# The MLP of a decoder layer in two phases, its down-projection as seven block products

## The chip, the cores and the metric

The kernel runs on one core of one Trainium2 chip. The metric is the device time of one execution in microseconds (us); 1 MB is a million bytes. Engine names are those of the profile: PE is TensorE, DVE is VectorE, ACT is ScalarE, POOL is GpSimd and SP is SyncE, which here issues almost all DMAs.

## What is computed

One layer of a decoder on x of 1024 tokens by 1024 features in float32: four token mixers, merged by gates and projected, are added to x, then the MLP is:

```
h = rms_norm(x, g_mlp) * (1 + sc2) + sh2          # (1024, 1024)
x = x + gt2 * (square(relu(h @ w_up)) @ w_down)   # w_up (1024, 4096), w_down (4096, 1024)
```

The change touches only the MLP. Below, u is square(relu(h @ w_up)), the hidden matrix.

## The kernel before

Every float32 product is made from two parts of each operand: a high part (ACT copies the float32 tile to fp32r, the format that PE reads) and a low part (operand minus high part, by DVE). `split_product` (L658) issues three matmuls for each pair of 128-row tiles: high by high, high by low, low by high, each with 128x128 weights and 512 moving columns.

All of the MLP is in `stage_close` (L676). The hidden features are cut into NB = 16 blocks of two tiles (BF = 2) of 128. For each block b there is an up-projection and a down-projection:

- Up, blocks 0 and 1 ("plain", 192 matmuls for both): a block's four results (feature tile f, token half h) are plain products.
- Up, blocks 2 to 15: seven products P1 to P7 take the place of eight (Winograd's form of Strassen's scheme), 12 matmuls each, 84 for a block. They need sums of w_up's quarters (`sum_units`, L1347, DVE, four 128x512 operations) and sums of h, made once (`difference`, nine DVE operations of 128x2048, and `low_difference`, four). `combine` (L1447) adds the products up from PSUM with five DVE operations.
- Down, every block: `down` (L1253) multiplies u's block by w_down's block as plain products, 16 groups (column half c, token tile tt) of 6 matmuls, 96 for a block. After each group `accumulate` (L1513) adds one 128x512 PSUM bank to x1, which is resident in SBUF. The gain gt2 is multiplied into w_down's tiles beforehand (`scale_unit`).

PE's order is: plain(0), plain(1), and then for b = 0..15 down(b) followed by up(b + 2) while there is one. The orders of ACT, DVE and SP are written out by hand to match. PSUM has eight banks; four serve the up products and four the down groups. w_up and w_down tiles of 256 KB pass through eight `unit` buffers, and their two parts through six slots. u stays in SBUF and is used by the next down(b). POOL does nothing in the MLP: its last work, the low parts of w_in's tiles (`Dense.low`, L137), ends before the MLP. SP stores each finished half row of x1 during the last block.

Of the kernel before, what the change touches and what calls it, by code (L numbers as in the profile page):

```python
# [675 lines left out]
def stage_close(nc, k, dense, w_br, x, w_out, w_up, w_down, out):  # L676
# [9 lines left out]
    with ExitStack() as ctx:  # L686

        def at(name, kb, shape, dt=F32):
# [33 lines left out]
        square = at("tl_square", 32, [P, BF, NH, HALF])  # L722
        first_product = at("tl_first_product", 216, [P, HALF])
        u_hi = [at("tl_u_hi", 48, [P, BF, S], F32R), at("tl_u_hi_last", 72, [P, BF, S], F32R)]
        u_lo = [at("tl_u_lo", 56, [P, BF, S], F32R), at("tl_u_lo_last", 80, [P, BF, S], F32R)]
        gain2 = at("tl_gain2", 40, [P, D])
        ps_y = ctx.enter_context(nc.psum_tensor("mg_ps_y", [P, Y_RING, NH, HALF], F32))
# [11 lines left out]
         turned, weighted, shifted, h_hi_ready, h_lo_ready, t_step, t_hi_ready, t_lo_ready, unit_scaled, unit_summed, slot_hi_ready, slot_lo_ready,  # L739
         up_done, taken, combined, relu_ready, square_ready, u_hi_ready, u_lo_ready, down_done, summed, out_stored) = sems(  # L740
# [3 lines left out]
                "t_lo_ready", "unit_scaled", "unit_summed", "slot_hi_ready", "slot_lo_ready", "up_done", "taken", "combined", "relu_ready",  # L744
                "square_ready", "u_hi_ready", "u_lo_ready", "down_done", "summed", "out_stored")))
# [3 lines left out]
        P1, P6, P5, P7, P2, P3, P4 = range(7)  # L749
        ITEMS = [("plain", b, (f, kh)) for b in range(PLAIN) for f in range(BF) for kh in range(2)]  # L750
        for b in range(NB):
            ITEMS += [("down", b, (c, f)) for c in range(NH) for f in range(BF)]
            if b + PLAIN < NB:
                ITEMS += [("up", b + PLAIN, (p,)) for p in range(7)]
        FIRST_DOWN = 4 * PLAIN
# [2095 lines left out]
```

## Time and profile before

| what | value |
|---|---|
| device time, median of three runs | 2024.57 us |
| the three runs | 2020.14, 2024.57, 2024.82 us |
| span of the profiled execution, first to last instruction | 2020.5 us |
| own device time of the profiled execution | not recorded beside its span |
| PE busy | 1967.2 us (97%), 9416 matmuls |
| DVE busy | 1264.0 us (63%) |
| ACT busy | 706.4 us (35%) |
| POOL busy | 227.3 us (11%) |
| DMA | 206.47 MB, mean 102 GB/s |

The span is that of one execution and is compared with spans of timelines; the runs are timed from outside it. Busy shares are averages over a program whose stages have different limits, so a share says little of the MLP by itself.

### The profile page before, as it was taken

The page shows a single profiled execution, that of the slowest core. Times are in us where ns is not written, and L with a number is a line of the kernel's source. Part 1 is how long each engine was busy: PE and PEld are TensorE (multiplying, and loading weights), DVE is VectorE, ACT ScalarE, POOL GpSimd, SP SyncE. Part 2 cuts the span into 40 slices and gives each one's busy share as a digit, 9 for nine tenths or more (in the row PEclk, how much of TensorE's full clock was granted, in tenths as well). Part 3 has the DMA queues.
Part 4 walks back from the last instruction along what each step waited for, and adds up shares of the span by engine and source line. Part 5 has one row for each costly group of instructions (what it writes and reads, how often), then busy time and mean ns, then how long its engine had stood idle before and what let it go on. Part 6 is the DMA issues. An engine that isn't in the chain of part 4 may idle for free. (4 is left out here: it accounts for less than half of the span.)

```text
span 2020.5 us, 24310 instructions
## 1 busy us (share of the span) xinstructions
PE 1967.2 (97%) x9416; PEld 1584.5 (78%) x9416; DVE 1264.0 (63%) x1655; ACT 706.4 (35%) x1100; POOL 227.3 (11%) x136
## 2 busy tenths in 40 slices
PE   5999999999999999999999999999999999999999
PEld 4787888878766677877788788787888888888887
DVE  6546666101356476548457587669877777777776
ACT  5411212123466542166654443333232122222221
POOL 0121212112222144121101000000000000000000
PEclk9999999999999999999998999999999999999999
DMA  8354554224311252353122765301111111211112
GB/s 275 96 150 144 160 153 141 89 83 123 123 58 47 68 169 58 105 209 120 47 75 83 257 229 182 115 11 59 57 52 60 47 47 48 68 48 48 48 42 94
DMA packets 197339, 206.47 MB, mean 102 GB/s; under 512 B 9402, under 2 KB 154938, under 8 KB 197226
## 3 DMA queue, kind: packets, MB, share of 16 engines
q1 hardware_dynamic: 197056, 204.85, 32.1%
q8 instruction: 76, 1.25, 0.3%
q14 instruction: 37, 0.30, 0.0%
q10 hardware_dynamic: 170, 0.07, 0.0%
HBM read 157.57 MB, written 47.32 MB: 101 GB/s over the span
## 5 line engine op out<-in xcount | busy, mean ns | idle before, releaser
L663 PE MATMUL dn_ps<-h_hi,dn_hi 128*128 128x512 f32 (+1 forms) x1120 | 453.0, 404 | 15.2 <-PEq L60 4.8
L665 PE MATMUL dn_ps<-h_hi,dn_lo 128*128 128x512 f32 (+1 forms) x1120 | 439.7, 393 | 0.0
L664 PE MATMUL dn_ps<-h_lo,dn_hi 128*128 128x512 f32 (+1 forms) x1120 | 439.5, 392 | 0.0
L663 PEld LDWEIGHTS dn_ps<-h_hi,dn_hi 128*128 128x128 f32 (+1 forms) x1120 | 210.5, 188 | 83.2 <-issue 32.6
L665 PEld LDWEIGHTS dn_ps<-h_hi,dn_lo 128*128 128x128 f32 (+1 forms) x1120 | 210.4, 188 | 47.6
L139 POOL TENSOR_TENSOR dn_lo<-dn_raw,dn_hi 128x1024 fp32r<-128x1024 f32 (+1 forms) x69 | 172.4, 2499 | 661.6 <-ACT dn_hi L135 661.6
L664 PEld LDWEIGHTS dn_ps<-h_lo,dn_hi 128*128 128x128 f32 (+1 forms) x1120 | 210.7, 188 | 43.2 <-issue 1.2
L1521 DVE TENSOR_TENSOR tl_x<-tl_x,mg_ps_y 128x512 f32<-128x512 f32 x256 | 176.0, 688 | 89.4 <-PE mg_ps_y L665 82.7
L156 ACT ACTIVATE dn_out<-dn_ps 128x512 f32<-128x512 f32 (+1 forms) x138 | 81.8, 592 | 422.7 <-PE dn_ps L665 401.6
L663 PE MATMUL mg_ps_y<-tl_slot_hi,tl_u_hi 128*128 128x512 f32 x480 | 187.1, 390 | 1.2 <-issue 1.2
L665 PE MATMUL mg_ps_y<-tl_slot_hi,tl_u_lo 128*128 128x512 f32 x480 | 186.9, 389 | 0.0
L664 PE MATMUL mg_ps_y<-tl_slot_lo,tl_u_hi 128*128 128x512 f32 x480 | 186.8, 389 | 0.0
L1021 ACT ACTIVATE tl_slot_hi<-tl_unit 128x512 fp32r<-128x512 f32 x128 | 77.7, 624 | 134.4 <-DVE tl_unit L1372 108.8
L555 DVE SCALAR_TENSOR_TENSOR ada_sum<-ada,cols,ada_sum 128x256 f32<-128x256 f32 (+1 forms) x140 | 105.6, 754 | 4.7
L663 PEld LDWEIGHTS mg_ps_y<-tl_slot_hi,tl_u_hi 128*128 128x128 f32 x480 | 90.1, 188 | 20.7 <-issue 2.0
L665 PEld LDWEIGHTS mg_ps_y<-tl_slot_hi,tl_u_lo 128*128 128x128 f32 x480 | 90.1, 188 | 18.7
L664 PEld LDWEIGHTS mg_ps_y<-tl_slot_lo,tl_u_hi 128*128 128x128 f32 x480 | 90.1, 188 | 18.6
L1377 DVE TENSOR_TENSOR tl_slot_lo<-tl_unit,tl_slot_hi 128x512 fp32r<-128x512 f32 x128 | 86.5, 689 | 24.8 <-ACT tl_slot_hi L1021 24.8
L1021 ACT ACTIVATE tl_slot_hi<-tl_unit_sum 128x512 fp32r<-128x512 f32 x42 | 26.5, 632 | 172.9 <-DVE tl_unit_sum L1360 146.9
L1071 ACT ACTIVATE tl_u_hi<-tl_square 128x512 fp32r<-128x512 f32 x60 | 33.3, 621 | 142.5 <-PE mg_ps_y L665 127.2
L561 DVE TENSOR_TENSOR mod<-ps_m,cols 128x2 f32<-128x2 f32 x24 | 3.5, 158 | 117.7 <-PE ps_m L474 117.7
L135 ACT ACTIVATE dn_hi<-dn_raw 128x1024 fp32r<-128x1024 f32 (+1 forms) x71 | 73.7, 1040 | 6.1 <-DMA dn_raw<-w_in_dram 6.1
(390 smaller groups left out, 3468.6 us busy)
## 6 DMA issues: line engine op xcount, KB each, us to landing
dn_raw<-w_in_dram SPq DMA_DIRECT2D x70, 512.0 KB, 4.4
ada<-w_ada_dram SPq DMA_DIRECT2D x24, 1024.0 KB, 7.9
proj<-dn_out SPq DMA_DIRECT2D x72, 256.0 KB, 2.3
logits<-dn_out SPq DMA_DIRECT2D x64, 256.0 KB, 2.3
tl_unit<-w_up_dram SPq DMA_DIRECT2D x64, 256.0 KB, 2.9
tl_unit<-w_down_dram SPq DMA_DIRECT2D x64, 256.0 KB, 2.8
mg_gate<-logits SPq DMA_DIRECT2D x19, 512.0 KB, 4.7
wa_qk<-proj SPq DMA_DIRECT2D x6, 1024.0 KB, 8.3
```

What stands on the lines that cost most here:

```text
L135: self.nc.scalar.activation(self.hi_at(j), self.raw_at(j), ACT.Copy).then_inc(self.hi_ready, 1)
L139: self.nc.gpsimd.tensor_tensor(self.lo_at(j), self.raw_at(j), self.hi_at(j).bitcast(F32), ALU.subtract).then_inc(self.lo_ready, 1)
L156: self.nc.scalar.activation(self.out[0:width, h, :], self.ps[0:width, h, :], ACT.Copy).then_inc(self.copied, 1)
L555: ins = nc.vector.scalar_tensor_tensor(out=total, in0=part, scalar=ck, in1=total, op0=ALU.mult, op1=ALU.add)
L561: last = nc.vector.tensor_tensor(k.mod[:, m:m + ADA_COLS], ps_m[:, m:m + ADA_COLS], k.cols[:, V_BADA + m:V_BADA + m + ADA_COLS], ALU.add)
L663: nc.tensor.matmul(out, w_hi[:, t, :], x_hi[:, t, :], start=begin, stop=False, skip_group_check=reopened)
L664: nc.tensor.matmul(out, w_hi[:, t, :], x_lo[:, t, :], start=False, stop=False, skip_group_check=reopened)
L665: mm = nc.tensor.matmul(out, w_lo[:, t, :], x_hi[:, t, :], start=False, stop=end, skip_group_check=reopened)
L1021: nc.scalar.activation(slot_hi[slot(j)][:, :, :], src, ACT.Copy).then_inc(slot_hi_ready, 1)
L1071: nc.scalar.activation(hidden_at(u_hi, b)[:, f, h * HALF:(h + 1) * HALF], square[:, f, h, :], ACT.Copy).then_inc(u_hi_ready, 1)
L1377: nc.vector.tensor_tensor(slot_lo[slot(j)][:, :, :], unit_at(kind, b, key), slot_hi[slot(j)][:, :, :].bitcast(F32), ALU.subtract).then_inc ...
L1521: nc.vector.tensor_tensor(x1[:, tt, cols], x1[:, tt, cols], bank(4 + n % 4), ALU.add).then_inc(summed, 1)
```

## The change

The MLP now runs in two phases, with a DRAM tensor `hidden` between them.

**Phase 1** is the whole up-projection, with no down groups between the blocks. PE goes from plain(1) straight to P1(2). The products of a block are issued in two parts, the second part (P2, P3, P4) one block later than the first, and two sets of four PSUM banks alternate by block. ACT makes the ReLU and the square (`finish`). DVE makes four sums S1 to S4 of each finished block's quarters (`sum_hidden`). SP stores three of the quarters and the four sums to `hidden` (`store_hidden`), seven tiles of 128x512 (256 KB each) a block.

**Phase 2** is the down-projection over u in two token halves and feature tiles in pairs, as seven block products for eight. Product i takes one of the seven stored matrices and one of w_down's quarters, of which some are turned in place into sums by DVE (`turn_down`, 64 operations). Each product has 16 steps, 112 steps in all, and a step is 4 token tiles by 3 matmuls. For step n:

- SP loads one 256 KB tile of `hidden` into one of three raw buffers, once the low part of step n - 3 is made, and loads the w_down cells that a later step needs.
- ACT makes both high parts, DVE the low part of the hidden tile, POOL the low part of the w_down cell. The parts sit in a ring of nine places, two for each step, so high parts may be made at most four steps ahead of PE.

PSUM is left only between products: ACT keeps three of them (`keep`), and DVE multiplies by gt2 and adds to x1 in `evict_down`, 60 operations in stretches of steps given by `EVICT_AT`, plus the last product at the end. `link` waits for the operation just issued. gt2's rows are saved to DRAM and read back in halves. There are no more `accumulate`, `scale_unit`, `square_relu` or `low_hidden` of the old kind.

The core of the diff:

```diff
+        RING_KB = (92, 208, 212, 16, 56, 60, 20, 44, 204)
+        ring_hi = [at(f"tl_ring_hi{i}", kb, [P, HALF], F32R) for i, kb in enumerate(RING_KB)]
+        raw_hidden = [at(f"tl_raw_hidden{i}", kb, [P, HALF]) for i, kb in enumerate((64, 66, 68))]
+        kept = at("tl_kept", 0, [P, 4, HALF])
...
+        for b in range(PLAIN, NB + 1):
+            ITEMS += [("up", b, (p,)) for p in FIRST_PART if b < NB]
+            ITEMS += [("up", b - 1, (p,)) for p in SECOND_PART if b > PLAIN]
...
+        DOWN = [(A11, W11), (A12, W21), (S2, W11), (S3, W12), (S1, W11), (S4, W22), (A22, W21)]
+        BY_EVEN = (0, 2, 3, 6)
+        STEPS = len(DOWN) * NB
+        LAST_STEPS = 4
+        SUMS_FROM = 14
...
+        NEEDS = sorted([(t, W11, t) for t in range(NB)] + [(NB + t, W21, t) for t in range(NB)]
+                       + [(SUMS_FROM + 2 * t, w, t) for t in range(NB) for w in (W22, W12)])
...
+        EVICT_AT = {36: (1, 0), 39: (1, 1), 42: (1, 2), 45: (1, 3), 52: (2, 0), 54: (2, 1), 56: (2, 2), 58: (2, 3),
+                    68: (3, 0), 71: (3, 1), 74: (3, 2), 77: (3, 3), 84: (4, 0), 86: (4, 1), 88: (4, 2), 90: (4, 3),
+                    100: (5, 0), 102: (5, 1), 104: (5, 2), 106: (5, 3)}
...
+            if m >= 9:
+                eng.wait_ge(step_done, (m - 9) // 2 + 1)
+            elif m in (4, 5):
+                eng.wait_ge(slot_lo_ready, PLACE["up", NB - 1, (P4,)] + 1)
...
+            def store_hidden(b):
+                sp.wait_ge(quad_ready[0], b + 1)
+                sp.dma_start(k.hidden[A11, b], square[b % 2][:, 0, 0, :]).then_inc(quads_stored[b % 2], 16)
+                sp.wait_ge(quad_ready[1], b + 1)
+                sp.wait_ge(quad_ready[3], b + 1)
+                sp.dma_start(k.hidden[A12:A22 + 1, b].rearrange("s p t -> p s t"), square[b % 2][:, 1]).then_inc(quads_stored[b % 2], 16)
+                sp.wait_ge(hidden_summed, 4 * (b + 1))
+                sp.dma_start(k.hidden[S1:S4 + 1, b].rearrange("s p t -> p s t"), hidden_sum[:, :, :]).then_inc(sums_stored, 16)
...
+                if n < 3:
+                    sp.wait_ge(slot_lo_ready, PLACE["up", NB - 2, (P3,)] + 1)
+                else:
+                    sp.wait_ge(ring_lo_ready, n - 2)
...
+            for b in range(PLAIN, NB):
+                if b >= PLAIN + 1 and b + 1 < NB:
+                    load_ups(b + 1)
+                store_hidden(b - PLAIN)
+            for n in range(3):
+                load_hidden(n)
+            loaded = 0
+            while loaded < 15:
+                load_cell(loaded)
+                loaded += 1
+            store_hidden(NB - 2)
+            load_gain(0)
+            for n in range(3, STEPS):
+                while loaded < len(NEEDS) and NEEDS[loaded][0] <= n + 2:
+                    load_cell(loaded)
+                    loaded += 1
+                if n == 9:
+                    store_hidden(NB - 1)
+                load_hidden(n)
+                if n == 30:
+                    load_gain(1)
+                if n in STORE_AT:
...
+            def high_hidden(n):
+                act.wait_ge(hidden_in[n % 3], 16 * (n // 3 + 1))
+                wait_ring(act, 2 * n)
+                nc.scalar.activation(ring_hi[2 * n % 9][:, :], raw_hidden[n % 3][:, :], ACT.Copy).then_inc(ring_hi_ready, 1)
...
+                wait_ring(act, 2 * n + 1)
+                nc.scalar.activation(ring_hi[(2 * n + 1) % 9][:, :], cell(w, t)[:, :], ACT.Copy).then_inc(cell_hi_ready, 1)
...
+            for n in range(3):
+                high_hidden(n)
+                high_cell(n)
+            finish(NB - 1, 0, 0)
+            high_hidden(3)
+            high_cell(3)
+            finish(NB - 1, 1, 0)
+            finish(NB - 1, 0, 1)
+            for n in range(4, STEPS):
+                high_hidden(n)
+                if n - 3 in (NB, 3 * NB, 5 * NB):
+                    keep((n - 3) // NB - 1)
+                high_cell(n)
 
         @block.gpsimd
...
+                pool.wait_ge(cell_hi_ready, n + 1)
+                r, own = (2 * n + 1) % 9, cell(DOWN[n // NB][1], n % NB)
+                nc.gpsimd.tensor_tensor(ring_lo[r][:, :], own[:, :], ring_hi[r][:, :].bitcast(F32), ALU.subtract).then_inc(cell_lo_ready, 1)
...
+            for n in range(STEPS):
+                low_cell(n)
...
+                pe.wait_ge(ring_lo_ready, n + 1)
+                pe.wait_ge(cell_lo_ready, n + 1)
+                a, w = 2 * n % 9, (2 * n + 1) % 9
+                return split_product(nc, down_bank(i, tt), ring_hi[a][:, cols].unsqueeze(1), ring_lo[a][:, cols].unsqueeze(1),
+                                     ring_hi[w][:, :].unsqueeze(1), ring_lo[w][:, :].unsqueeze(1), first=(t == 0 and i not in (2, 3, 5)),
+                                     last=(t == NB - 1), reopened=i in (2, 3, 5))
...
+            for n in range(STEPS - LAST_STEPS):
+                for tt in range(4):
+                    last = down(n, tt)
+                    if n % NB == NB - 1 and tt < 3:
+                        last.then_inc(bank_done, 1)
+                last.then_inc(step_done, 1)
+            for tt in range(4):
+                for n in range(STEPS - LAST_STEPS, STEPS):
+                    last = down(n, tt)
+                last.then_inc(bank_done if tt < 3 else step_done, 1)
...
+                elif i == 3 and part == 0:
+                    link(nc.vector.tensor_tensor(product, own, g0, ALU.mult))
+                elif i == 3 and part == 1:
+                    link(nc.vector.tensor_tensor(rows[2], rows[2], product, ALU.subtract))
+                elif i == 3 and part == 2:
+                    nc.vector.tensor_tensor(other, own, g1, ALU.mult).then_inc(even_read, 1)
+                    dve.wait_ge(even_read, tt + 1)
+                elif i == 3 and part == 3:
+                    link(nc.vector.tensor_tensor(rows[3], rows[3], other, ALU.subtract))
...
+            for n in (1, 2, 3):
+                difference(n)
             for kh in range(2):
                 low_slot("plain", 1, (0, kh))
+            for n in (4, 5):
+                difference(n)
             for kh in range(2):
                 low_slot("plain", 1, (1, kh))
             low_difference(0)
             difference(6)
             difference(7)
             difference(8)
+            low_difference(1)
+            for n in (1, 2, 3):
+                sum_units(PLAIN, n)
+            for p in (P1, P6):
+                low_slot("up", PLAIN, (p,))
+            low_difference(2)
+            sum_units(PLAIN, 4)
+            for p in (P5, P7):
+                low_slot("up", PLAIN, (p,))
             difference(9)
+            low_difference(3)
+            for b in range(PLAIN, NB + 1):
+                if b > PLAIN:
+                    low_slot("up", b - 1, (P2,))
+                if b > PLAIN + 1:
+                    combine(b - 2, 5)
+                    combine(b - 2, 4)
+                if b > PLAIN:
+                    low_slot("up", b - 1, (P3,))
+                    low_slot("up", b - 1, (P4,))
+                if b < NB:
+                    combine(b, 1)
+                sum_hidden(b - 2)
+                if b + 1 < NB:
+                    for n in (1, 2, 3):
+                        sum_units(b + 1, n)
+                    for p in (P1, P6):
+                        low_slot("up", b + 1, (p,))
+                    sum_units(b + 1, 4)
+                    for p in (P5, P7):
+                        low_slot("up", b + 1, (p,))
+                if b < NB:
+                    combine(b, 2)
+                    combine(b, 3)
+            for n in range(3):
+                low_hidden(n)
+            combine(NB - 1, 5)
+            combine(NB - 1, 4)
+            low_hidden(3)
+            sum_hidden(NB - 1)
+            for n in range(4, STEPS):
+                where = EVICT_AT.get(n)
+                if where:
+                    evict_down(*where, 0)
+                if 0 <= n - SUMS_FROM < 4 * NB:
+                    turn_down(n - SUMS_FROM)
+                if where:
+                    evict_down(*where, 1)
+                low_hidden(n)
+                if where:
+                    evict_down(*where, 2)
+                if where:
+                    evict_down(*where, 3)
+            for tt in range(4):
+                evict_down(6, tt, 0)
+                evict_down(6, tt, 1)
```

## Rows read from the trace of the kernel before

**Rows 1.** The page: busy time and share of the engines; granted clock by slice.
```profile
PE 1967.2 (97%) x9416; PEld 1584.5 (78%) x9416; DVE 1264.0 (63%) x1655; ACT 706.4 (35%) x1100; POOL 227.3 (11%) x136
...
PEclk9999999999999999999998999999999999999999
```

**Rows 2.** Who PE waited for, from 1300 us to the end.
```profile
PE mg_ps_y L1208 <- DVE tl_xn L1397: 2.1, 2, 1.5
PE mg_ps_y L663 <- issue: 1.2, 1, 1.2
```

**Rows 3.** Timeline of PE, end of the plain products, and the last matmul: start, duration.
```profile
1395.83 0.39 PE L665 MATMUL mg_ps_y<-tl_h_hi,tl_slot_lo 128*128 128x512 f32 x1
...
1400.59 0.39 PE L665 MATMUL mg_ps_y<-tl_h_hi,tl_slot_lo 128*128 128x512 f32 x1
1400.82 0.39 PE L663 MATMUL mg_ps_y<-tl_slot_hi,tl_u_hi 128*128 128x512 f32 x1
...
2016.97 0.39 PE L665 MATMUL mg_ps_y<-tl_slot_hi,tl_u_lo_last 128*128 128x512 f32 x1
```

**Rows 4.** Groups from 1380 us on: count, busy us and mean ns, idle before.
```profile
L1377 DVE TENSOR_TENSOR tl_slot_lo<-tl_unit,tl_slot_hi 128x512 fp32r<-128x512 f32 x122 | 82.6, 689 | 24.8 <-ACT tl_slot_hi L1021 24.8
L1021 ACT ACTIVATE tl_slot_hi<-tl_unit 128x512 fp32r<-128x512 f32 x122 | 74.2, 625 | 134.4 <-DVE tl_unit L1372 108.8 <-PE mg_ps_y L665 25.5
...
L1057 ACT ACTIVATE tl_square<-dn_ps 128x512 f32<-128x512 f32 x16 | 9.2, 579 | 0.0
L1445 DVE TENSOR_TENSOR tl_t_lo<-tl_t_full,tl_t_hi 128x2048 fp32r<-128x2048 f32 x4 | 9.1, 2287 | 0.0
```

**Rows 5.** Timeline of DVE after the last tile of h: start, duration.
```profile
1367.63 0.68 DVE L1478 TENSOR_TENSOR tl_square<-tl_square 128x512 f32<-128x512 f32 x1
1368.23 2.29 DVE L1425 TENSOR_TENSOR tl_t_full<-tl_h_hi 128x2048 f32<-128x2048 f32 x1
1370.43 2.29 DVE L1427 TENSOR_TENSOR tl_t_full<-tl_h_lo 128x2048 f32<-128x2048 f32 x1
```

**Rows 6.** Timeline of ACT, the ReLUs that follow plain products: start, duration, idle before.
```profile
1379.25 0.60 ACT L1057 ACTIVATE tl_square<-mg_ps_y 128x512 f32<-128x512 f32 x1 [1.26 <-PE mg_ps_y L665]
...
1398.30 0.60 ACT L1057 ACTIVATE tl_square<-mg_ps_y 128x512 f32<-128x512 f32 x1 [2.50 <-PE mg_ps_y L665]
```

**Rows 7.** Timelines of POOL (first) and DVE, 782 to 805 us.
```profile
782.69 2.40 POOL L139 TENSOR_TENSOR dn_lo<-dn_raw,dn_hi 128x1024 fp32r<-128x1024 f32 x1 [3.45 <-ACT dn_hi L135]
...
803.17 2.41 POOL L139 TENSOR_TENSOR dn_lo<-dn_raw,dn_hi 128x1024 fp32r<-128x1024 f32 x1 [3.45 <-ACT dn_hi L135]
...
783.10 3.08 DVE L2435 TENSOR_TENSOR gl_parts<-gl_k,gl_dist 128x1024 f32<-128x1024 f32 x1
...
793.40 1.21 DVE L2435 TENSOR_TENSOR gl_parts<-gl_k,gl_dist 128x1024 f32<-128x1024 f32 x1
...
803.72 2.94 DVE L2435 TENSOR_TENSOR gl_parts<-gl_k,gl_dist 128x1024 f32<-128x1024 f32 x1
```

**Rows 8.** The tile dn_lo: durations in ns, least, median, most.
```profile
L139 POOL TENSOR_TENSOR dn_lo<-dn_raw,dn_hi x69: 459/2400/4467, 80.2 to 1126.9; 128x1024 fp32r<-128x1024 f32 x68, 128x128 fp32r<-128x128 f32 x1
```

**Rows 9.** DMA issues: KB each, median us to landing; then landing at L917, least, median, most.
```profile
tl_unit<-w_down_dram SPq DMA_DIRECT2D x64, 256.0 KB, 2.8
...
out_dram<-tl_x SPq DMA_DIRECT2D x16, 256.0 KB, 2.0
...
DMA to landing us min/median/max: 2.3/2.8/8.9
```

**Rows 10.** Two stretches of 10 us; the last columns are clock, DMA share, GB/s.
```profile
10.00:20.00 10.00, 6.04 (x25) 4.88 (x25) 6.76 (x11) 6.54 (x17) 0.00 (x0) 1.00 1.09 355
1130.00:1140.00 10.00, 10.00 (x45) 8.26 (x44) 5.15 (x5) 3.81 (x5) 0.00 (x0) 1.00 0.96 315
```

**Rows 11.** Timeline of DVE, its last operation.
```profile
2017.40 0.69 DVE L1521 TENSOR_TENSOR tl_x<-tl_x,mg_ps_y 128x512 f32<-128x512 f32 x1 [0.67 <-PE mg_ps_y L665]
```

More of the change, by code:

```diff
@@ L749, in stage_close @@
         P1, P6, P5, P7, P2, P3, P4 = range(7)
+        FIRST_PART, SECOND_PART = (P1, P6, P5, P7), (P2, P3, P4)
         ITEMS = [("plain", b, (f, kh)) for b in range(PLAIN) for f in range(BF) for kh in range(2)]
[L751 to L755, printed above, removed]
-        PLACE = {item: j for j, item in enumerate(ITEMS)}
+        FIRST_UP = len(ITEMS)
@@ L757, in stage_close @@
+        STORE_AT = [n + 3 for n, (i, tt) in EVICT_AT.items() if i in (1, 4, 5)]
+        gain_half = [at("tl_gain_half0", 40, [P, HALF]), cells[len(NEEDS)]]
         QUADS = [(0, 0), (1, 0), (0, 1), (1, 1)]
@@ new lines, in wait_cell_free, with load_cell @@
+            def wait_cell_free(i):
+                kb, kind, key = CELLS[i]
+                if kind == "up":
+                    sp.wait_ge(up_done, up_count(NB - 1, key))
+                elif kind == "slot":
+                    sp.wait_ge(slot_lo_ready, PLACE["up", key[0], (key[1],)] + 1)
+                else:
+                    sp.wait_ge(quads_stored[key % 2], 32 * (key // 2 + 1))
+                    sp.wait_ge(hidden_summed, 4 * (key + 1))
+            def load_cell(i):
+                need, w, t = NEEDS[i]
+                wait_cell_free(i)
+                if i >= 8:
+                    sp.wait_ge(down_in[i % 8], 16 * (i // 8))
+                row, column = (2 * t + w // 2) * P, w % 2 * HALF
+                sp.dma_start(cells[i][:, :], w_down[0, row:row + P, column:column + HALF]).then_inc(down_in[i % 8], 16)
@@ L1073, in high_difference @@
+                nc.scalar.activation(first_product[b % 2][:, :], bank_of(b, 0), ACT.Copy).then_inc(taken, 1)
             def high_difference(i):
@@ new lines, in wait_down_bank @@
+            def wait_down_bank(i, tt):
+                if i in (0, 1):
+                    b = NB - 2 + i
+                    pe.wait_ge(clipped[0], nth(b))
+                    for n in (0, 3, 4):
+                        pe.wait_ge(combined[n], nth(b))
+                elif i in (2, 3, 5):
+                    pe.wait_ge(kept_ready, {2: 0, 3: 4, 5: 8}[i] + tt + 1)
+                elif i == 4:
+                    pe.wait_ge(odd_read, tt + 1)
+                else:
+                    pe.wait_ge(even_read, tt + 1)
@@ L1513, in accumulate, with sum_hidden @@
-            def accumulate(b, c, tt):
-                n = (b * NH + c) * TT + tt
-                cols = slice(c * HALF, (c + 1) * HALF)
-                dve.wait_ge(down_done, n + 1)
+                    nc.vector.tensor_tensor(own[:, 1, 0, :], u2, bank_of(b, 3), ALU.add).then_inc(combined[4], 1)
+            def sum_hidden(b):
+                a11, a21, a12, a22 = (square[b % 2][:, f, h, :] for f in range(BF) for h in range(NH))
+                s1, s2, s3, s4 = (hidden_sum[:, n, :] for n in range(4))
+                for q in range(4):
+                    dve.wait_ge(quad_ready[q], b + 1)
@@ L1639 @@
+            for tt in range(4):
+                evict_down(6, tt, 0)
+                evict_down(6, tt, 1)
 UNIT_STEP = (1, 4, 8)
@@ L2795, in build @@
     k.window = nc.dram_tensor("window", (2, S, ROW), F32, kind="Internal").ap()
+    k.hidden = nc.dram_tensor("hidden", (7, NB, P, HALF), F32, kind="Internal").ap()
+    k.gain = nc.dram_tensor("gain", (P, D), F32, kind="Internal").ap()
     k.mix = nc.dram_tensor("mix", (Y_TILES * P, S), F32, kind="Internal").ap()
```

539 lines of the change are left out of this document (283 added, 256 removed).

## The prediction

> **What bounds the kernel now.** I read the page first: PE is busy for 97% of the span at full granted clock in the last slices [rows 1]. Then the waits of PE: from 1300 us to the end they sum to 3.3 us [rows 2]. So the MLP is PE's own stream, and its price is the number of matmuls. The timeline of PE gives the pace: 21 matmuls from 1395.83 to 1400.59, 0.2267 us each, and from 1400.82 to 2016.97 the 2712 matmuls of the other up blocks and of all down groups take 616.15 us, 1.4 us more than 2711 such intervals (614.6) [rows 3]. A matmul taken away there is worth 0.227 us, as long as nothing else comes to end last. The other rows are for that condition.
>
> **The stream of PE.** Down before: 16 blocks x 16 groups x 6 = 1536 matmuls. After: 112 steps x 12 = 1344. The up products stay 192 + 14 x 84. So 192 fewer x 0.2267 = **-43.5 us**. A step lasts 12 x 0.2267 = 2.72 us, a block of phase 1 84 x 0.2267 = 19.0 us, one of its products 2.72 us.
>
> **The start of phase 1.** Before, the nine differences, their low parts and the weights of P1(2) to P7(2) were made beside down(0). Now P1(2) may start at 1400.8, when the plain products end, and P1(3) four products later, at 1411.7. DVE is free at 1367.6, where its first square stood [rows 5]. From there to the low part of P1(3) its list has 13 operations of 128x2048 and 21 of 128x512. The first kind follows one another after 2.20 us [rows 5]; the second after 0.60 (1367.63 to 1368.23 [rows 5]). That is 28.6 + 12.6 = 41.2 us, ending at 1408.8, if DVE waits for nothing. It does wait for ACT, whose list is also in order: for the splits of plain 1's second pair behind the squares after the ReLU of 1379.25 (1.5 us), for P5(2)'s and P7(2)'s high parts behind the last two ReLUs and squares, of which one can only start at 1401 (3.8 us; before, a ReLU waited so at 1398.30 [rows 6]), and for the last high difference (2 us). So P1(3) is ready at about 1416.1, **+4.4 us**; bounds 0 (no waits) and 6 (two-step differences that wait for their own result). P1(2), P6(2), P5(2) and P7(2) are in time, by my count of the same list at 1395.6, 1396.2, 1403.5 and 1404.1, against 1400.8, 1403.5, 1406.3 and 1409.0.
>
> **Phase 1 in its stride.** For each block DVE has 7 low parts, 5 combines, 4 sums of the hidden, 4 of the units: 20 x 0.60 to 0.69 = 12 to 14 us of 19.0 [rows 4, 5]. ACT has 16 operations of at most 0.63, 10 us [rows 4]. SP moves 11 tiles of 256 KB, 2.9 MB in 19 us or 152 GB/s, below half of what the queues have carried [rows 10]. Walking one block through, P2(b)'s weights are ready some 12 us early and the others more than 3. Cost nothing; the cover is 5 us of idle DVE a block.
>
> **The hand-over.** Let T be the start of P1(15) and T' = T + 19.0 the start of P2(15); phase 2 may start at T' + 8.2. Here SP's queue is the matter. At T + 8.6, when block 13's sums are made, 7 tiles are stored, 3 hidden tiles and 15 cells are loaded: 25 x 0.262 = 6.6 MB. Then come block 14's seven tiles and a half of gt2, 2.1 MB, issued at T' + 6.2, and only behind them the hidden tile of step 3. The queues carried 355 GB/s at best and 315 in another busy stretch [rows 10]; I take 330, between them: 20 us, to T' + 9.5, then 6.4 us, to T' + 15.9, and 2.3 for the tile itself (a 256 KB load lands after 2.3 at least [rows 9]). With 0.62 on ACT and 0.69 on DVE [rows 4] step 3 is ready at about T' + 19.4, where PE wants it at T' + 16.3: +3.1. Step 4 then waits for block 15: ACT's cell, four ReLUs and squares (0.58 each [rows 4]), DVE's four sums, one low part, to about T' + 24.6, against T' + 22.1: +2.5. Together **+5.5 us**; bounds 0 (355 GB/s, and the stores beside the loads) and 12 (at 275 GB/s both transfers take 5 us more).
>
> **Phase 2, the loads.** Up to step 13 and from step 32 they are light. Between, each step brings one hidden tile and two cells, 0.79 MB in 2.72 us or 290 GB/s, under the 315 and 355 seen [rows 10]. A raw buffer turns round in landing + 0.62 + 0.69; at 2.8 [rows 9] that is 4.1 us for three steps, at 5 us under load 6.3, against 8.2. Cost 0; upper bound 8 us.
>
> **Phase 2, POOL and DVE.** POOL's subtraction of 128x1024 takes 2.40, the one of 128x128 0.46 [rows 8]; of 128x512 then 1.20 (half) to 1.29 (on the line through both). That is under 2.72. But the two disturb each other: DVE's product of two SBUF tiles takes 1.21 alone and 3.08 or 2.94 when it starts 0.4 or 0.55 after a POOL subtraction of 2.40, and it ends 1.1 after POOL's end [rows 7]. So I add their times. A step from 14 to 77 has two such DVE operations and one of POOL: 2 x 0.60 + 1.20 = 2.40 to 2 x 0.69 + 1.29 = 2.67. That fits, barely. The three stretches of evictions that fall in it don't: steps 36 to 47 add 12 operations, 52 to 59 8, 68 to 79 16, each behind `link` at 0.69. At 2.40 a step DVE falls behind by 4.5 + 2.9 + 6.0 = 13.4 us and makes good 0.32 in each of the 12 steps between, 9.6 in all; the 12 evictions that read PSUM may run beside POOL, which gives back up to 8.3. At 2.67 the deficit is 21. Against this DVE may lead PE by 4 steps less ACT's two operations and its own, 10.9 - 1.9 = 9 us. So I take 0; bounds 0 and 12.
>
> The Trainium skill (SBUF — State Buffer, section "Who interferes with whom") states that a DVE instruction with two SBUF inputs and a GpSimd one that reads SBUF exclude each other for the whole instruction. By this the split of work between the two engines saves nothing of their sum; the trace agrees (3.08 = 2.0 of waiting + 1.1). The sum stands at 0 or at the bound of 12 by it, depending on the lead.
>
> **ACT and the banks.** ACT has 2 x 0.63 of 2.72 us a step; the copies that keep products 0, 2 and 4 (four of 0.6) run behind the last step of a product, tile by tile, one group of 3 matmuls (0.68) each, so the next product finds its banks read about 1 us early. Cost 0, bound 2.
>
> **The end.** After the last matmul there are now a product and a sum in place of one sum [rows 11], **+0.7**; the store (2.0 [rows 9]) stays.
>
> **Sum.** -43.5 + 4.4 + 5.5 + 0.7 = **-32.9 us**. The profiled execution has no own time beside its span of 2020.5, which would become 1987.6; the median of the runs is 4.1 above the span, and I take it as the base: 2024.6 - 32.9 = **1991.7**. The lowest run, 2020.1, would give 1987.2.
>
> **Rivals.**
> - *POOL and DVE's lock.* The evictions use up the lead, and PE waits in steps 36 to 80, by the row of 3.08 [rows 7]. For it: the bases of 2.40 to 2.67 leave little. Against: the lead and the PSUM reads. +7 (up to 12): 1999. Chance 0.17. The rule named above is this rival's.
> - *The burst of transfers.* Stores and loads mixed run at 275 or less, or steps 14 to 31 use up the ring. +11: 2003. Against: the 355. Chance 0.11.
> - *The round of the hidden tile, slower than before.* SP issues it only after the low part three steps back, ACT splits it behind a wait, DVE behind its evictions. Where a tile lands after 8.9 us, the most seen at that line [rows 9], the round takes 8.9 + 0.62 + 0.69 = 10.2 for three steps, 3.4 a step in place of 2.72: 112 x 0.68 = +76, **2068**. It decides from a mean landing of about 7.7 us on, where 112 x 0.29 = 33 eats the gain. Against: the median of 2.8, and 7.7 would be needed over the whole phase, not only in the 16 busy steps. Chance 0.04.
> - *Both hand-overs covered.* ACT's waits smaller and the stores fast: 2024.6 - 43.5 + 1 = 1982. Chance 0.07.
>
> That fewer products are issued than I count can't be: the loops fix 112 x 12.
>
> **Chances.** The forecast has 0.58, from 1985 to 1997. Something of several of these that ends within 0.3% of before (2018.5 to 2030.6; what a measurement of this kernel can tell from none) has 0.03. Faster is 0.58 + 0.17 + 0.11 + 0.07 = 0.93, slower 0.04. The range takes in the covered case from the lower run and the two rivals: 1982 to 2004.
>
> **What would show it.** PE with 9224 matmuls and 0.2267 us between two; one gap near 1412 that ends on DVE's low part of P1(3); one or two before steps 3 and 4, ending on DVE's low part, behind a load of `hidden` that lands late; none after. POOL's operation 1.2 to 1.9 us, DVE's two-SBUF ones 0.69 to 1.9. If PE's waits in phase 2 lie on POOL or DVE in steps 36 to 80, the first rival holds; if evenly on DVE behind the DMA, the third; a pace of over 0.23 us with no waits would break the first term.

## The result and the profile after

The changed kernel takes 1993.98 us (median of four runs, 1990.49 to 1995.49) beside 2022.36 us for the one before (four runs, 2020.0 to 2024.82): ratio 0.9852, 95% interval 0.9836 to 0.9868. It is faster by 28 us. The profiled execution took 1995.01 us with a span of 1993.3.

The page of the changed kernel, beside [rows 1]:

```profile
PE 1928.5 (97%) x9224; PEld 1551.1 (78%) x9224; DVE 1209.5 (61%) x1443; ACT 831.2 (42%) x1314; POOL 386.0 (19%) x248
...
PEclk7999999999999999999998999999999999999999
```

192 matmuls are gone and PE still fills the span. Who PE waited for, from 1300 us to the end, beside the 3.3 us of [rows 2] (total, times, longest):

```profile
PE mg_ps_y L663 <- DVE tl_slot_lo L1567: 6.3, 2, 4.5
PE dn_ps L663 <- DVE tl_ring_lo L1703: 3.7, 2, 3.5
PE mg_ps_y L1385 <- DVE tl_xn L1587: 2.1, 2, 1.5
PE dn_ps L663 <- POOL tl_ring_lo L1340: 0.2, 1, 0.2
```

The third line is work ahead of the MLP, as before. The others are 10.2 us, and three gaps make 9.8 of it. The timeline of PE places them (start, duration, and in brackets the idle time before):

```profile
1401.14 0.39 PE L663 MATMUL dn_ps<-tl_h_hi,tl_slot_hi 128*128 128x512 f32 x1
...
1416.64 0.79 PE L663 MATMUL mg_ps_y<-tl_h_hi,tl_slot_hi 128*128 128x512 f32 x1 [4.46 <-DVE tl_slot_lo L1567]
1417.23 0.63 PE L664 MATMUL mg_ps_y<-tl_h_lo,tl_slot_hi 128*128 128x512 f32 x1
1417.66 0.63 PE L665 MATMUL mg_ps_y<-tl_h_hi,tl_slot_lo 128*128 128x512 f32 x1
...
1671.36 0.50 PE L663 MATMUL mg_ps_y<-tl_h_hi,tl_slot_hi 128*128 128x512 f32 x1 [1.81 <-DVE tl_slot_lo L1567]
...
1688.15 0.39 PE L665 MATMUL mg_ps_y<-tl_ring_hi,tl_ring_lo 128*128 128x512 f32 x1
1692.01 0.80 PE L663 MATMUL dn_ps<-tl_ring_hi,tl_ring_hi 128*128 128x512 f32 x1 [3.48 <-DVE tl_ring_lo L1703]
...
1989.01 0.39 PE L665 MATMUL mg_ps_y<-tl_ring_hi,tl_ring_lo 128*128 128x512 f32 x1
```

The first gap stands before P1(3). The second stands before P3(15), the last product but one of phase 1. The third stands before step 4 of phase 2. Behind the first and the third the matmuls start 0.43 us apart (1417.23 to 1417.66) where it is 0.2267 elsewhere: the clock is at its lower level there. Stretches of the changed kernel (us, then busy time of PE, PEld, DVE, ACT, POOL, then granted clock, DMA share, GB/s):

```profile
1404.00:1411.00 7.00, 7.00 (x33) 5.79 (x32) 5.02 (x4) 2.92 (x3) 0.00 (x0) 1.00 0.00 0
1417.00:1420.00 3.00, 3.00 (x8) 2.33 (x8) 2.97 (x6) 1.21 (x3) 0.00 (x0) 0.50 0.70 194
1423.00:1426.00 3.00, 3.00 (x15) 2.49 (x14) 1.61 (x4) 1.94 (x4) 0.00 (x0) 1.00 0.77 233
1660.00:1680.00 20.00, 17.91 (x79) 14.18 (x78) 11.45 (x15) 10.59 (x19) 4.85 (x3) 1.00 0.97 340
1693.00:1696.00 3.00, 3.00 (x8) 2.32 (x7) 0.75 (x2) 1.15 (x2) 0.03 (x1) 0.50 0.92 315
1760.00:1960.00 200.00, 200.00 (x885) 165.68 (x884) 168.53 (x170) 88.98 (x156) 105.51 (x74) 1.00 0.42 122
```

A granted clock of 0.50 is 1.2 GHz, 1.00 is 2.4. In 3 us at 1.00 PE starts 13 matmuls, at 0.50 it starts 7 (the rows also count those that already run at their start). Counted over PE's whole list, 10 matmuls behind the first gap and 13 behind the third start late by 0.2 us each: 4.6 us. In the last line PE is busy for all of 200 us with no wait.

**Where the time went.** Ahead of the MLP the profiled executions of this document differ by up to 5.7 us (the first matmul of P1(2) starts between 1397.8 and 1403.5), so I compare the stretch from the first matmul of P1(2) (before: of the first down group) to the end of the span. Before: 2020.5 - 1400.8 = 619.7. After: 1993.3 - 1401.1 = 592.2. The terms of the 27.5 us are -43.5 for the matmuls, +4.5 for the start of phase 1, +6.3 for the hand-over (its working is below), +4.6 for the half clock and +0.8 for the tail: from the last matmul to the end it is 4.3 us where it was 3.5. They sum to -27.3. Two small things are left out and cancel: PE's single gap of before, at 1409 (the 1.2 us of "issue" in [rows 2], 1.5 us beyond its pace in all), is gone, and the starts next to the gaps of the changed kernel lose some 1.4 us more.

DVE's timeline ahead of the first gap, where the low part of P1(3) is the last of these lines:

```profile
1408.63 2.29 DVE L1635 TENSOR_TENSOR tl_t_lo<-tl_t_full,tl_t_hi 128x2048 fp32r<-128x2048 f32 x1 [1.98 <-ACT tl_t_hi L1213]
1410.84 0.68 DVE L1644 TENSOR_TENSOR tl_first_product<-tl_first_product,dn_ps 128x512 f32<-128x512 f32 x1
...
1415.90 0.68 DVE L1567 TENSOR_TENSOR tl_slot_lo<-tl_unit,tl_slot_hi 128x512 fp32r<-128x512 f32 x1
```

The **first gap** is DVE's order. From 1410.84 to 1415.90 DVE works without a pause, on a combine, block 0's four sums and three sums of w_up's quarters. None of it is an operand of P1(3), whose high part ACT had finished at 1409.6.

The hand-over in the timelines of the changed kernel. DVE:

```profile
1670.62 1.29 DVE L1567 TENSOR_TENSOR tl_slot_lo<-tl_unit,tl_slot_hi 128x512 fp32r<-128x512 f32 x2 [2.46 <-ACT tl_slot_hi L1153]
...
1675.35 4.06 DVE L1703 TENSOR_TENSOR tl_ring_lo<-tl_raw_hidden,tl_ring_hi 128x512 fp32r<-128x512 f32 x3
...
1685.62 0.69 DVE L1671 TENSOR_TENSOR tl_hidden_sum<-tl_square 128x512 f32<-128x512 f32 x1 [2.26 <-ACT tl_square L1199]
...
1686.83 1.79 DVE L1674 TENSOR_TENSOR tl_hidden_sum<-tl_square,tl_hidden_sum 128x512 f32<-128x512 f32 x1
1688.65 1.63 DVE L1676 TENSOR_TENSOR tl_hidden_sum<-tl_square,tl_hidden_sum 128x512 f32<-128x512 f32 x1
```

ACT:

```profile
1669.97 1.13 ACT L1153 ACTIVATE tl_slot_hi<-tl_unit 128x512 fp32r<-128x512 f32 x2
...
1682.01 0.63 ACT L1218 ACTIVATE tl_ring_hi<-tl_raw_hidden 128x512 fp32r<-128x512 f32 x1 [5.45 <-DMA tl_raw_hidden<-hidden]
```

POOL, and then SP's queue:

```profile
1686.65 4.76 POOL L1340 TENSOR_TENSOR tl_ring_lo<-tl_cell,tl_ring_hi 128x512 fp32r<-128x512 f32 x3 [2.12 <-ACT tl_ring_hi L1228]
```

```profile
1677.15 6.56 SPq L1007 DMA_DIRECT2D tl_raw_hidden<-hidden  x4
```

The **second gap** is ACT's order: at 1669.97 it splits the units of P3(15) and P4(15), but only behind the ReLUs and squares of block 14. The **third gap** is a chain. SP issues the hidden tile of step 3 at 1677.15, once DVE has made the low part of step 0 behind block 14's sums. It lands 4.8 us later. The tile itself is in time for step 3, which PE starts at 1685.65 without a wait. But ACT has sat 5.45 us in front of it, and behind it in ACT's list stand the last quarters of block 15. They reach DVE at 1685.62, and DVE makes the sums while POOL works: 1.79 and 1.63 us in place of 0.69. Only then comes the low part of step 4.

### The profile page after: what moved, and what is told of

Read it like the earlier page. It is cut to its first block and busy times, and to the rows that moved or that the text cites. A ratio compares the mean times of both kernels' runs of the same rounds, so it can differ in the third digit from the quotient of the medians.

```text
span 1993.3 us, 24602 instructions
## 1 busy us (share of the span) xinstructions
PE 1928.5 (97%) x9224; PEld 1551.1 (78%) x9224; DVE 1209.5 (61%) x1443; ACT 831.2 (42%) x1314; POOL 386.0 (19%) x248
## 5 line engine op out<-in xcount | busy, mean ns | idle before, releaser
L1340 POOL TENSOR_TENSOR tl_ring_lo<-tl_cell,tl_ring_hi 128x512 fp32r<-128x512 f32 x112 | 158.3, 1415 | 692.2 <-ACT tl_ring_hi L1228 692.2
L1703 DVE TENSOR_TENSOR tl_ring_lo<-tl_raw_hidden,tl_ring_hi 128x512 fp32r<-128x512 f32 x112 | 140.1, 1255 | 63.5 <-ACT tl_ring_hi L1218 63.0
L1228 ACT ACTIVATE tl_ring_hi<-tl_cell 128x512 fp32r<-128x512 f32 x112 | 70.6, 631 | 151.9 <-PE mg_ps_y L665 144.1
L664 PE MATMUL mg_ps_y<-tl_ring_lo,tl_ring_hi 128*128 128x512 f32 x320 | 125.1, 391 | 0.0
L663 PE MATMUL mg_ps_y<-tl_ring_hi,tl_ring_hi 128*128 128x512 f32 x320 | 125.1, 391 | 0.0
L665 PE MATMUL mg_ps_y<-tl_ring_hi,tl_ring_lo 128*128 128x512 f32 x320 | 125.1, 391 | 0.0
L664 PE MATMUL mg_ps_y<-tl_t_lo,tl_slot_hi 128*128 128x512 f32 x196 | 76.3, 389 | 0.0
L665 PE MATMUL mg_ps_y<-tl_t_hi,tl_slot_lo 128*128 128x512 f32 x196 | 76.3, 389 | 0.0
L663 PE MATMUL mg_ps_y<-tl_t_hi,tl_slot_hi 128*128 128x512 f32 x196 | 76.3, 389 | 0.0
L1218 ACT ACTIVATE tl_ring_hi<-tl_raw_hidden 128x512 fp32r<-128x512 f32 x112 | 69.1, 617 | 16.5 <-DMA tl_raw_hidden<-hidden 16.5
```

The lines of the kernel that those rows point to most:

```text
L663: nc.tensor.matmul(out, w_hi[:, t, :], x_hi[:, t, :], start=begin, stop=False, skip_group_check=reopened)
L664: nc.tensor.matmul(out, w_hi[:, t, :], x_lo[:, t, :], start=False, stop=False, skip_group_check=reopened)
L665: mm = nc.tensor.matmul(out, w_lo[:, t, :], x_hi[:, t, :], start=False, stop=end, skip_group_check=reopened)
L1218: nc.scalar.activation(ring_hi[2 * n % 9][:, :], raw_hidden[n % 3][:, :], ACT.Copy).then_inc(ring_hi_ready, 1)
L1228: nc.scalar.activation(ring_hi[(2 * n + 1) % 9][:, :], cell(w, t)[:, :], ACT.Copy).then_inc(cell_hi_ready, 1)
L1340: nc.gpsimd.tensor_tensor(ring_lo[r][:, :], own[:, :], ring_hi[r][:, :].bitcast(F32), ALU.subtract).then_inc(cell_lo_ready, 1)
```

## The experiments

The diffs are against the changed kernel, the fifth against the kernel before. "Stretch" is the stretch of the MLP as above. Each ratio goes by runs of the kernel before from the same batch: a median of 2024.28 us for runs 1 to 4, 2022.98 for runs 5 to 8 and 2022.99 for run 9.

**1. The changed kernel again**, no edit, for the scatter.

> The changed kernel itself, as the yardstick for the other three of this call, on the same chip. Expected: 28 us (26 to 30) under the kernel before, with one PE gap of about 4.5 us near 1412 us, one of 1.8 us near 1670, one of 3.5 us near 1688, and two stretches of 6.8 us at the granted clock of 0.5 right behind the first and the last gap. If the clock stretches are an accident of one execution, this profile will not have them.

Measured: 1991.63 us (1991.41 to 1996.47), ratio 0.985 (0.9832 to 0.9869), stretch 591.4. The same three gaps stand there, 4.5, 1.8 and 3.5 us, and 4.1 us of late starts at half clock. What the gaps cost is a property of the program, not of one execution.

**2. The start of phase 1.** The last difference of h with its high and low part, a combine and block 0's sums go behind the low parts of P1(3) to P7(3). Not shown below are the move of the high part in ACT's list and a wait that DVE's new order needs.

```diff
-            difference(9)
-            low_difference(3)
...
-                if b < NB:
+                if PLAIN < b < NB:
                     combine(b, 1)
-                sum_hidden(b - 2)
+                if b > PLAIN:
+                    sum_hidden(b - 2)
...
+                if b == PLAIN:
+                    difference(9)
+                    combine(b, 1)
+                    sum_hidden(0)
...
+                if b == PLAIN:
+                    low_difference(3)
```

> Only the start of phase 1 is reordered: the ninth difference and its two parts, combine 1 and sum_hidden(0) are put behind the low parts of P1(3) to P7(3). Theory A (the gap of 4.5 us near 1412 is DVE's backlog, and the stretch of 6.8 us at half clock that follows costs another 3.4): PE has no gap there and no half clock, and the time is 7.9 us under the changed kernel. Rival B (the half clock has nothing to do with the gap): 4.5 us under it, with the half clock still there. Rival C (the work put back makes P4(2) or P2(2) late): a gap of 2 us or more some 20 us later, and a gain under 3.

Measured: 1986.53 us (1984.97 to 1987.82), ratio 0.9817 (0.9803 to 0.9832), stretch 583.5, so 7.9 us shorter. PE's waits of this kernel:

```profile
PE dn_ps L663 <- DVE tl_ring_lo L1706: 3.7, 2, 3.5
PE mg_ps_y L1386 <- DVE tl_xn L1590: 2.1, 2, 1.5
PE mg_ps_y L663 <- DVE tl_slot_lo L1570: 1.8, 1, 1.8
```

The gap of 4.5 is gone and no other has come. The rest of the 7.9 is the clock: the late starts fall from 4.1 us to 1.0. Those behind the first gap are gone with it (1.6), and of those before step 4 only 5 matmuls are left for 13, though that gap is unchanged. How many matmuls a gap of 3.5 us slows down thus differs between executions, and nothing ties these 1.6 of the 7.9 us to the edit.

**3. The hand-over.** The slots of P3(15) and P4(15) are split ahead of block 14's finish and combines, and block 15's last quarters and sums go behind the hidden parts of steps 4 to 6:

```diff
+                if b == NB:
+                    split_slot("up", b - 1, (P3,))
+                    split_slot("up", b - 1, (P4,))
...
-            high_hidden(3)
-            high_cell(3)
+            for n in range(3, 6):
+                high_hidden(n)
+                high_cell(n)
...
-            low_hidden(3)
+            for n in range(3, 7):
+                low_hidden(n)
             sum_hidden(NB - 1)
```

> Only the hand-over is reordered: in the last up block the slots of P3(15) and P4(15) are split before block 14's last quarters are finished (the gap of 1.8 us), and block 15's last two quarters and its sums are made behind the hidden parts of steps 4 to 6 instead of ahead of step 4 (the gap of 3.5). Theory A (both gaps are places in a list, and the half clock follows from the gap): no gaps at 1670 and 1688, no half clock, 1.8 + 3.5 + 0.2 + 3.4 = 8.9 us under the changed kernel. Rival B (the gap before step 4 is the DMA burst: the hidden tile of step 3 lands late whatever stands behind it): gain under 3, and PE waits before step 4, 5 or 9 with ACT waiting for a hidden tile.

Measured: 1987.37 us (1985.55 to 1990.62), ratio 0.9824 (0.9808 to 0.9839), stretch 587.1, 4.3 us shorter. That is half of the 8.9 expected. Both gaps of the hand-over are gone, and one of 2.0 us has come before step 9:

```profile
1698.45 0.75 PE L663 MATMUL dn_ps<-tl_ring_hi,tl_ring_hi 128*128 128x512 f32 x1 [2.01 <-POOL tl_ring_lo L1344]
```

ACT's timeline shows its head, another tile of `hidden`:

```profile
1695.81 0.63 ACT L1218 ACTIVATE tl_ring_hi<-tl_raw_hidden 128x512 fp32r<-128x512 f32 x1 [9.23 <-DMA tl_raw_hidden<-hidden]
```

SP has block 15's store in its list ahead of the tile of step 9, that store waits for block 15's sums, and the sums are now later. A wait was moved past a queue that I had not moved with it: part of the gain was turned into a new wait. The clock took more of it back. Behind this gap of 2.0 us 7 matmuls start late (granted clock 0.52 from 1699 to 1702), and 11 behind the first gap, 3.6 us in all beside 4.1 in run 1.

**4. The cells' low parts on DVE**, none on POOL:

```diff
-            for n in range(STEPS):
-                low_cell(n)
...
+                dve.wait_ge(cell_hi_ready, n + 1)
+                r, own = (2 * n + 1) % 9, cell(DOWN[n // NB][1], n % NB)
+                nc.vector.tensor_tensor(ring_lo[r][:, :], own[:, :], ring_hi[r][:, :].bitcast(F32), ALU.subtract).then_inc(cell_lo_ready, 1)
```

> The low parts of the w_down cells are made by DVE right behind the low part of the hidden tile, and POOL makes none. Theory A (POOL's operation and DVE's two-SBUF operations exclude each other, so POOL's 1.29 us are taken from DVE anyway): DVE's operations go back to 0.69 us each, its list has three of 0.60 a step in place of two and a wait of up to 1.3, nothing is late in phase 2, and the time is that of the changed kernel or 1 to 3 us less (the sums of block 15 are no longer slowed from 0.69 to 1.7). Rival B (POOL takes work off DVE that DVE has no room for): PE waits for DVE in the eviction stretches from step 36 to 80, and the time is 5 to 20 us above the changed kernel.

Measured: 1987.26 us (1985.6 to 1989.74), ratio 0.9822 (0.9808 to 0.9837), stretch 585.8, 5.6 us shorter. That is more than the 1 to 3 us expected. The gap before step 4 has shrunk from 3.5 us to 0.7, since the sums take 0.69 each again, and no new wait has come. The rest is the clock: behind step 4 no matmul starts late, where 13 did. The low parts, first in the changed kernel (least, median and most in ns), then here:

```profile
L1340 POOL TENSOR_TENSOR tl_ring_lo<-tl_cell,tl_ring_hi x112: 1279/1295/1805, 1673.4 to 1978.9; 128x512 fp32r<-128x512 f32 x112
L1703 DVE TENSOR_TENSOR tl_ring_lo<-tl_raw_hidden,tl_ring_hi x112: 678/1360/1806, 1675.3 to 1976.6; 128x512 fp32r<-128x512 f32 x112
```

```profile
L1696 DVE TENSOR_TENSOR tl_ring_lo<-tl_raw_hidden,tl_ring_hi x112: 682/685/694, 1671.6 to 1967.7; 128x512 fp32r<-128x512 f32 x112
```

The stretch of 200 us at the same place of phase 2 as 1760 to 1960 above:

```profile
1756.80:1956.80 200.00, 200.00 (x884) 165.68 (x883) 153.94 (x244) 89.39 (x156) 0.00 (x0) 1.00 0.41 121
```

DVE does 244 operations here for 170, and is busy for 154 us in place of 168.5. With POOL's help it had been busier than without.

**5. The kernel before with 192 matmuls fewer.** It leaves out the product of the high part of u with the low part of w_down in the groups of column half 1 from token tile 2 on. Nothing else is changed, so it prices the first term alone.

```diff
+            def down_product(out, w_hi, w_lo, x_hi, x_lo, first, last, short):
+                nc.tensor.matmul(out, w_hi, x_hi, start=first, stop=False)
+                if not short:
+                    nc.tensor.matmul(out, w_hi, x_lo, start=False, stop=False)
+                return nc.tensor.matmul(out, w_lo, x_hi, start=False, stop=last)
...
-                                          flat(slot_hi[slot(j)]).unsqueeze(1), flat(slot_lo[slot(j)]).unsqueeze(1), first=(f == 0), last=(f == BF - 1))
+                                        flat(slot_hi[slot(j)]), flat(slot_lo[slot(j)]), f == 0, f == BF - 1, c == 1 and tt >= 2)
```

> The kernel before with 192 of its down-projection's matmuls left out and nothing else: in 6 of the 16 groups of each block, high hidden by low w_down is not multiplied. All transfers, splits and additions stay. Theory (the first term of the sum: 192 matmuls at 0.2267 us, on a PE stream that nothing else holds up): 43.5 us under the kernel before, that is 1979 to 1981, no new waits of PE. Rival (before's DVE or another engine is close behind PE, so the matmuls are worth less): gain of 30 or less, with PE waiting for DVE.

Measured: 1980.29 us (1977.64 to 1984.99, five runs), ratio 0.9792 (0.9775 to 0.9809): -42.7 us beside the kernel before, and its stretch of 578.1 is 41.6 us shorter. At 0.2267 us they were to be 43.5. PE's waits from 1400 us on are the 1.2 us of "issue" that were there before and 0.5 us for DVE, so no other engine holds PE's stream up by more than that. The matmuls are thus worth nearly all of their pace, and the changed kernel falls short of this one by 14 us: what the two phases cost.

**6. POOL makes each low part twice**, to see where its load decides:

```diff
+                nc.gpsimd.tensor_tensor(ring_lo[r][:, :], own[:, :], ring_hi[r][:, :].bitcast(F32), ALU.subtract).then_inc(pool_twice, 1)
+                pool.wait_ge(pool_twice, n + 1)
```

> The changed kernel with POOL making each low part twice. Theory A (POOL and DVE's two-SBUF operations exclude each other): a step from 14 to 77 needs 2 x 0.60 on DVE and 2 x 1.2 to 1.29 on POOL one after the other, 3.6 to 3.8 us against PE's 2.72, so the time is 60 to 80 us above the changed kernel, nearly all of it in steps 14 to 77, while steps 0 to 13 and 80 to 111, with one DVE operation, cost 3.0 to 3.2 a step at the most. Rival B (POOL has its own 2.72 us a step, of which 2.6 are used): no more than 5 us.

Measured: 2073.29 us (2069.91 to 2075.23), ratio 1.0249 (1.0233 to 1.0265), about 80 us over the changed kernel, the top of what was expected. The largest of PE's waits, and a stretch of phase 2:

```profile
PE dn_ps L663 <- DVE tl_ring_lo L1706: 14.9, 8, 3.3
PE dn_ps L663 <- POOL tl_ring_lo L1343: 11.9, 22, 1.6
PE mg_ps_y L663 <- POOL tl_ring_lo L1343: 11.2, 28, 0.4
```

```profile
1720.00:1760.00 40.00, 35.44 (x144) 25.64 (x142) 40.00 (x24) 15.61 (x27) 39.06 (x24) 1.00 0.73 235
```

Both engines are full, with 24 operations each in 40 us. A step outside the evictions has here two operations of POOL and two of DVE and takes 3.40 us:

```profile
1763.73 0.47 PE L663 MATMUL mg_ps_y<-tl_ring_hi,tl_ring_hi 128*128 128x512 f32 x1 [0.39 <-POOL tl_ring_lo L1343]
1767.13 0.47 PE L663 MATMUL mg_ps_y<-tl_ring_hi,tl_ring_hi 128*128 128x512 f32 x1 [0.39 <-POOL tl_ring_lo L1343]
```

Side by side the four would take 2 x 1.29 = 2.6, and PE's 2.72 would still end last. One after the other, with DVE's at 0.60 (their spacing in [rows 5]) and POOL's at 1.29, they would take 3.78. The 3.40 is much nearer to that sum, but 0.38 short of it: by my estimate some 0.2 us of each operation of POOL runs beside DVE after all. So the times add up, but for this part. From step 14 to 77 a step takes 3.60 in the mean (3.99 in the evictions of steps 36 to 47), as expected; but the later steps are longer too, 3.13 from step 80 to 106, so that only some 56 of the 78.5 us by which the stretch has grown lie in steps 14 to 77, and not nearly all.

**7. All orders changed**: 2 and 3 together, and block 15's quarters stored at step 10, its sums at step 13, behind the tiles that the ring needs:

```diff
-                if n == 9:
-                    store_hidden(NB - 1)
+                if n == 10:
+                    store_quads(NB - 1)
+                if n == 13:
+                    store_sums(NB - 1)
```

> The start and the hand-over both reordered, and besides block 15's quarters are stored before the load of step 10 and its sums before that of step 13, in place of all before step 9 (in e3 they held back the hidden tile of step 9, and PE waited 2.0 us). Theory A: no gap of PE from 1400 us on and no half clock behind one, so 43.5 - 0.7 = 42.8 less than the kernel before but for 1 to 2 us: 1977 to 1981. Rival B (each gap that is closed opens another, as in e3): PE still waits 3 us or more, now before a step from 9 to 15, and the time is 1983 or more.

Measured: **1976.41 us** (1975.91 to 1982.23), ratio 0.9778 (0.9761 to 0.9795), stretch 576.9, 14.5 us shorter. All of PE's waits from 1300 us on:

```profile
PE mg_ps_y L1403 <- DVE tl_xn L1607: 2.1, 2, 1.5
PE dn_ps L663 <- DVE tl_ring_lo L1723: 0.6, 1, 0.6
PE dn_ps L663 <- POOL tl_ring_lo L1358: 0.2, 1, 0.2
```

The gap of run 3 is gone with its cause, and the clock stays at its upper level through the MLP: one matmul starts late. This kernel beats both: by 47 us the one before, by 15 the changed one of run 1. Its stretch is even 1.2 us shorter than that of run 5, which has as many matmuls and the old order: the two phases need cost nothing.

**8. The same with the cells' low parts on DVE** (7 and 4 together).

> The same as e7, with the low parts of the cells made by DVE and none by POOL. Theory A: with no gap left in e7 there is nothing for it to win: within 1 us of e7. Rival B (POOL's share slows things in ways that the waits don't show, or DVE becomes late in the eviction stretches): 3 us or more apart from e7, either way.

Measured: 1978.22 us (1976.15 to 1979.91, five runs), ratio 0.9784 (0.977 to 0.9797), stretch 575.2. PE has no wait of the MLP. The 2519 intervals between its 2520 matmuls are 571.1 at 0.2267, and a tail of 4.3 from the start of the last makes 575.4: the stretch holds nothing else. The intervals of runs 7 and 8 overlap, so once the orders are right, POOL's work costs nothing that the time shows.

**9. Only the slots of P3(15) and P4(15) first**, the first three added lines of run 3's edit, on ACT and on DVE.

> Only one thing of the hand-over is changed: ACT and DVE split the slots of P3(15) and P4(15) ahead of the finish and the combines of block 14. Block 15's sums before step 4 stay as they are in the changed kernel. Theory A (each gap has its own cause): the gap of 1.8 us near 1669 goes, the one of 3.5 us before step 4 stays within 0.5 us of that, so does the stretch at half clock behind it, and the stretch of the MLP is 1 to 2.5 us shorter than in the changed kernel run again (591.4). Theory B (a wait removed is given back later): block 14's finish and combines come later by as much, DVE reaches block 15's sums later, and the gap before step 4 grows by 1.8 us to about 5.3; the stretch stays at 591 to 592.

Measured: 1990.92 us (1989.87 to 1991.63), ratio 0.9844 (0.9828 to 0.9861), stretch 589.1, 2.3 us shorter. PE's timeline:

```profile
1689.14 0.50 PE L663 MATMUL dn_ps<-tl_ring_hi,tl_ring_hi 128*128 128x512 f32 x1 [4.34 <-DVE tl_ring_lo L1706]
```

The gap of 1.8 us is gone and the one before step 4 has grown from 3.5 to 4.3. Each theory was half right. PE arrives at step 4 earlier by the whole gap, but the chain that ends there by only a part of it. Counted from the start of P2(15), SP issues the hidden tile of step 3 after 7.9 us here and after 10.5 in the changed kernel, but the tile then needs 5.9 us in place of 4.8. From the start of P2(15) to step 4 it is 23.7 us here and 25.3 in the changed kernel, where PE's own work is 19.0.

## Why the prediction was right, and where its terms were off

The forecast was 1991.7 us in 1982 to 2004, against 1993.98. In the MLP's own stretch it said -32.9 and the trace says -27.5. That the time itself is only 2.3 us off is in part luck: the base of 2024.6 was 2.2 us above the median of the four runs before, and from there the kernel gained 28.4 us and not 32.9.

- **The stream of PE, -43.5: right.** Pace and count came as worked out (9224 matmuls), and run 5 measures 42.7 by the time and 41.6 by the stretch for the matmuls alone. (616.15 is 1.5 us more than 614.6, and not 1.4.)
- **The start of phase 1, +4.4: right, 4.46.** P1(3) was to be ready at 1416.1; DVE begins its low part at 1415.90, and PE starts at 1416.64. Run 2 shows the cause, the items that stand in front of it. It also shows that this cover was free to have: nothing else became late.
- **Phase 1 in its stride, 0: right** up to block 14. At its end the count missed the slots of P3(15) and P4(15): with no further first part between, ACT reaches them too late, 1.81 us.
- **The hand-over, +5.5: near in its end, partly wrong on the way.** The prediction had step 4 at T' + 24.6, with T' the start of P2(15). T' was 1666.7 and step 4 began at 1692.0, T' + 25.3. Without waits it is 7 x 2.72 = 19.0 later, so the term measured 6.3, in which the 1.8 us before P3(15) are counted. That the chain runs through the late tile of step 3, block 15's last quarters and its sums was as put. But the gap forecast before step 3 (+3.1) did not come. The queues carried 340 GB/s from 1660 to 1680, and the tile's high part began at T' + 15.3 and not after T' + 18.2. The 2.9 us gained there were lost again on DVE: the sums and the low part were priced at 0.60 to 0.69, and POOL stretched two of the sums to 1.79 and 1.63 and the low part as well. From the tile's high part to step 4 it was 10.0 us where 6.4 were forecast. That the two errors cancel to 0.7 is luck. Run 4 takes the stretching away: the 10.0 become 7.6, and step 4 comes at 1685.9 with T' at 1663.9, so T' + 22.1, 3.2 us earlier. The slots of P3(15) and P4(15) have a part in this chain too, for in run 9, which moves only them, step 4 comes at T' + 23.7. The step at fault is that I counted the lock between DVE and POOL for the stretches of evictions alone, where there was a lead, and not for the one place without one.
- **Phase 2, the loads, 0: right.** PE has no wait in it after step 4.
- **Phase 2, POOL and DVE, 0 with a bound of 12: right as a number.** The rival of the lock describes what happens: in run 4 the operation of DVE that takes 1360 ns beside POOL takes 685, and in run 6 a step takes 3.40 us. The Trainium skill (SBUF — State Buffer, section "Who interferes with whom") puts it down to ports that the two engines share by an exclusive lock. Runs 4 and 6 agree in the main, but the step of 3.40 is 0.38 us less than full exclusion would give. In steps 36 to 80, though, the lead held, and PE never waited there. The price came out elsewhere, before step 4.
- **The tail, +0.7: right, 0.8.**
- **The missing term: the half clock, 4.6 us in the profiled execution.** No sentence of the prediction asks what PE's clock does behind a wait. [rows 1] had only full clock in the last slices, and in the MLP no gap of more than 1.2 us stood there to show it. It is most of the 5.4 us by which the stretch is longer than forecast; the hand-over is 0.8.

Of the rivals, the burst of transfers falls with 340 GB/s, and the round trip of the hidden tile as well: it would show as waits all through phase 2, and there are none. "Both hand-overs covered" (1982) did not occur, but runs 7 and 8 show that it can be had, and better than forecast: 1976.4.

What stays open: why one gap of 3.5 us is followed by 13 slow matmuls and the same gap in another execution by 5. And the executions differ by up to 5.7 us ahead of the MLP. Stretches of half clock stand there too, but they don't explain it: the execution of run 3 has more of them than that of run 6 and reaches the MLP 5 us earlier. No experiment here concerns this.

## What to carry to other kernels

When one engine bounds a long stretch, price removed work by its pace, then walk every in-order list (ACT, DVE, SP, POOL) through each place where one phase hands over to the next: work that isn't due yet, standing ahead of work that is, cost some 14 us of the 43 here, with the waits and the clock behind them, and changing orders alone brought it back (run 7). Count each such gap with the time at half clock that can follow it. And before a part of DVE's two-input work is given to POOL, add their times up: here DVE alone was less busy than DVE with help.

## What the runs showed of the hardware that was not expected

- After PE had stood still for 4.46 and 3.48 us, its granted clock fell from 1.00 (2.4 GHz) to 0.50 (1.2 GHz), and 23 matmuls started 0.43 us apart in place of 0.2267. A stand of 2.01 us in run 3 was followed by 7 such matmuls, those of 1.81 us by none. Without the gaps (run 8) none did. So the wait of 4.46 us cost 1.6 to 2.4 us more behind it, in each of the six profiles that have it.
- A subtraction of 128x512 takes POOL 1.29 us in the median, 1.28 at least. Beside it, DVE's operation with two SBUF inputs goes from 0.69 to 1.36 in the median and to 1.81 at most, POOL's to 1.81 at most too: the cost falls on both.
- Mixed loads and stores moved 340 GB/s over 20 us (1660 to 1680), and 378 from 1660 to 1680 in run 9, where the best stretch of [rows 10] had 355.
